# Long self-attention units: two exponential instructions each, and the causal mask added by VectorE

## The reference, cut to what matters

```python
sc = jnp.einsum('bqhd,bkhd->bhqk', qi, k).astype(jnp.float32) * scale
mask = kpos[None, :] <= qpos[:, None]
sc = jnp.where(mask[None, None], sc, -jnp.inf)
p = jax.nn.softmax(sc, axis=-1).astype(v.dtype)
return jnp.einsum('bhqk,bkhd->bqhd', p, v)
```

## Time and profile before

| what | value |
|---|---|
| median of three runs | 2906.83 us |
| the profiled execution | 2907.68 us |
| its span, first to last instruction | 2905.5 us |
| TensorE matmuls, busy | 2851.7 us, 98% |
| VectorE busy | 1533.3 us, 53% |
| ScalarE busy | 860.8 us, 30% |
| GpSimd busy | 1555.7 us, 54% |
| mean granted TensorE clock | 0.998 |
| attention stage of the first layer | about 197 to 405 us of the span |
| attention stage of the second layer | about 1634 to 1843 us |

### The profile page before, as it was taken

The page is one execution under the profiler, slowest core; times in us unless marked ns, Lnnn a source line. Parts: engine busy times, 40 slices in busy tenths (PEclk is TensorE's granted clock), DMA queues, the critical chain, the costliest instruction groups (busy, mean ns, idle before and its releaser), DMA issues.

```text
span 2905.5 us, 36839 instructions
## 1 busy us (share of the span) xinstructions
PE 2851.7 (98%) x13294; PEld 2224.1 (77%) x13294; DVE 1533.3 (53%) x1949; ACT 860.8 (30%) x1440; POOL 1555.7 (54%) x1153
## 2 busy tenths in 40 slices
PE   8999999999999999999999999999999999999998
PEld 6766668886878888888887666688878788888886
DVE  8585556014565445554685755650246555545555
ACT  3455553223321111110224655432324111101113
POOL 4333333441487777777644224334315877777776
PEclk9999999999999999999999999999999999999999
DMA  3100011220111111111111000113101111111112
GB/s 135 48 10 5 16 37 51 87 88 15 44 44 58 47 41 56 58 47 43 60 61 37 14 1 16 44 51 109 59 22 44 40 54 58 51 43 50 58 54 77
DMA packets 61423, 140.37 MB, mean 48 GB/s; under 512 B 9232, under 2 KB 11280, under 8 KB 60688
## 3 DMA queue, kind: packets, MB, share of 16 engines
q1 hardware_dynamic: 61328, 139.06, 14.2%
HBM read 134.58 MB, written 4.46 MB: 48 GB/s over the span
## 4 chain that ended last, share of the span: by engine, by line
PE 86%; DVE 6%; POOL 3%; ACT 2%; issue 2%; DMA 1%; SPq 0%; POOLq 0%; DVEq 0%; ACTq 0%
PE ps L1357 23%; PE ps L1341 19%; PE ps L845 17%; PE ps L1213 6%; PE ps L1067 4%; PE ps L1097 2%; PE ps L1269 2%; PE ps L1293 2%; PE ps L1083 2%; PE ps L1228 1%; PE ps L961 1%; PE ps L1244 1%; DVE xbc L1852 1%; PE ps L1163 1%; POOL ring L751 1%
## 5 line engine op out<-in xcount | busy, mean ns | idle before, releaser
L1357 PE MATMUL ps<-hm_h,ring 128*128 128x512 f32 x2048 | 640.8, 391 | 4.5 <-DVE hm_l L2171 4.4
L2179 DVE TENSOR_TENSOR x<-ps,x 128x512 f32<-128x512 f32 x512 | 352.3, 690 | 273.9 <-PE ps L1357 273.3
L748 POOL TENSOR_TENSOR ring<-raw,ones 128x512 fp32r<-128x512 f32 x334 | 349.9, 1048 | 260.6 <-PE ps L1357 204.3
L1357 PEld LDWEIGHTS ps<-hm_h,ring 128*128 128x128 f32 x2048 | 384.5, 188 | 96.9 <-issue 16.5
L751 POOL TENSOR_TENSOR ring<-raw,ring 128x512 fp32r<-128x512 f32 x334 | 433.1, 1297 | 26.1
L845 PE MATMUL ps<-hA,wsp 128*128 128x512 f32 x1920 | 443.2, 392 | 1.1 <-POOL wsp L603 1.0
L600 POOL TENSOR_TENSOR wsp<-raw,ones 128x1024 fp32r<-128x1024 f32 x63 | 124.4, 1974 | 566.7 <-PE ps L845 454.6
L845 PEld LDWEIGHTS ps<-hA,wsp 128*128 128x128 f32 x1920 | 360.4, 188 | 82.0 <-issue 6.3
L1357 PE MATMUL ps<-hm_l,ring 128*128 128x512 f32 x1024 | 398.9, 390 | 0.0
L1341 PE MATMUL ps<-hT,ring 128*128 128x512 f32 x1440 | 331.9, 390 | 0.9 <-POOL ring L751 0.7
L1341 PEld LDWEIGHTS ps<-hT,ring 128*128 128x128 f32 x1440 | 270.3, 188 | 57.6 <-POOL ring L751 1.7
(11 more groups left out here) (308 smaller groups left out, 3940.2 us busy)
## 6 DMA issues: line engine op xcount, KB each, us to landing
raw<-in_weight_tiles SPq DMA_DIRECT2D x248, 256.0 KB, 2.6
raw<-in_weight_tiles SPq DMA_DIRECT2D x108, 512.0 KB, 3.2
outT<-x SPq DMA_DIRECT2D x16, 256.0 KB, 2.2
x<-in_xT SPq DMA_DIRECT2D x3, 1024.0 KB, 10.2
wh<-in_head_weights SPq DMA_DIRECT2D x8, 256.0 KB, 2.7
raw_early<-in_weight_tiles SPq DMA_DIRECT2D x4, 512.0 KB, 3.7
mem_s<-in_memT SPq DMA_DIRECT2D x2, 1024.0 KB, 4.8
x<-in_xT SPq DMA_DIRECT2D x2, 512.0 KB, 5.3
```

Source lines behind the costliest of these rows:

```text
L748: pool.tensor_tensor(ring[:, slot, 0, :], blk(i), ones[:, 0:1].to_broadcast([P, HT]), ALU.mult).then_inc(op_ready[slot], 1)
L1357: last = pe.matmul(ps[:, bank, :], w[:, part, k, (m % 2) * P:(m % 2 + 1) * P], h[k][:, cols_of(half)], start=(k == 0 and part == 0 and h i ...
L2179: dve.tensor_tensor(xm, ps[:, bank, :], xm, ALU.add).then_inc(x_add, 1)
```

## The change: what it does

It touches the long units alone.

- `scores`: the mask's product (L1070) is left out for them.
- `row_max`: VectorE first adds `future` to the diagonal square in PSUM, 128 by 128, in place, and then (after a `link`) reduces.
- `probs`: the first 512 columns and the rest are two ACTIVATEs. The first sums into a new tile `esum_4` and raises a new semaphore `s_exp_4`; the second sums into `esum` and raises `s_exp`.
- `probs_T`: the first chunk (4 squares) of a long unit waits for `s_exp_4`, the second for `s_exp`.
- `recip_sums`: for the long half of the blocks the two partial sums are first added (128 by 8) and linked.

```diff
+def long_units(n):
+    return sum(unit(m)[1] >= 4 for m in range(n))
...
         esum_4 = at("esum_4", G2 + 4096, [P, 2, NBLK // 2])
...
-                            edge = j + 4 > i
+                            edge = j + 4 > i and i < 4
...
-                        pe.wait_ge(s_exp, here(s_exp, n + 1))
                         for part, j0 in enumerate(range(0, i + 1, 4)):
+                            if part == 0 and i >= 4:
+                                pe.wait_ge(s_exp_4, here(s_exp_4, long_units(n + 1)))
+                            else:
+                                pe.wait_ge(s_exp, here(s_exp, n + 1))
...
-                        act.activation(prob[:, n % 2, 0:w], banks(2 * (n % 2))[:, 0:w], ACT.Exp,
+                        first = 0
+                        if w > HT:
+                            first = HT
+                            act.activation(prob[:, n % 2, 0:HT], ps[:, 2 * (n % 2), :], ACT.Exp,
+                                           bias=stat(nmx, n), accum_out=stat(esum_4, n)).then_inc(s_exp_4, 1)
+                        act.activation(prob[:, n % 2, first:w], banks(2 * (n % 2))[:, first:w], ACT.Exp,
                                        bias=stat(nmx, n), accum_out=stat(esum, n)).then_inc(s_exp, 1)
...
                         w = (unit(n)[1] + 1) * P
+                        diagonal = banks(2 * (n % 2))[:, w - P:w]
+                        if unit(n)[1] >= 4:
+                            link(dve.tensor_tensor(diagonal, diagonal, future[:, :], ALU.add))
                         dve.tensor_reduce(stat(nmx, n), banks(2 * (n % 2))[:, 0:w], AX.X, ALU.max, negate=True).then_inc(s_max, 1)
...
                         dve.wait_ge(s_exp, here(s_exp, 8 * hf + 8))
+                        if hf % 2:
+                            link(dve.tensor_tensor(esum[:, :, 4:NBLK], esum[:, :, 4:NBLK], esum_4[:, :, :], ALU.add))
```

More of the change, by code:

```diff
@@ L172 @@
              "softplus_a": 2, "norm_done": 3, "bc_done": 6, "act_done": 8, "gate_done": 4, "lru_a": 4, "first_qk_act": 8,
-             "k_rope": 2, "k_rope_1": 2, "v_done": 8, "s_exp": 64, "side_act": 42, "pt_sb": 96, "mix_hi": 6, "mix_ln": 1, "mix_gt": 4, "mix_rstd": 3, "mg_hi": 1,
+             "k_rope": 2, "k_rope_1": 2, "v_done": 8, "s_exp": 64, "s_exp_4": 32, "side_act": 42, "pt_sb": 96, "mix_hi": 6, "mix_ln": 1, "mix_gt": 4, "mix_rstd": 3, "mg_hi": 1,
              "xk_done": 8, "mv_done": 2, "xs_exp": 8, "xpt_sb": 8, "xo_hi": 16, "sum_y": 4, "sum_hi": 16, "hm_sq": 64,
@@ L337, in trunk @@
         att_h = at("att_h", o + 824, [P, NBLK, SH], F32R)
+        esum_4 = at("esum_4", G2 + 4096, [P, 2, NBLK // 2])
         cst_r = sem("constants_r")
@@ L376, in trunk @@
         s_ps, s_max, s_exp, pt_ps, pt_sb, o_ps = (sem(n) for n in ("s_ps", "s_max", "s_exp", "pt_ps", "pt_sb", "o_ps"))
+        s_exp_4 = sem("s_exp_4")
         r_inv, y_done, y_sq, y_acc = sem("r_inv"), sem("y_done"), sem("y_sq"), sem("y_acc")
```

## The result

The changed kernel takes 2925.01 us, the median of four runs (2923.49 to 2925.45), against 2906.36 for the kernel before measured beside it: a ratio of 1.006, 95% interval 1.0048 to 1.0072. The forecast was 2919.3, in 2909 to 2927, slower. So direction and range held, and the size was 12.5 us where 18.65 came. The profiled execution took 2923.49 us; its span is 2921.2, 15.7 over the span before.

What follows compares the result with a forecast made beforehand. TensorE bounds the kernel, through its waits on ScalarE's copies behind the exponential. Per layer 3 x 1.31 + 2.32 = 6.25 us, two layers 12.5, giving a median of 2919.3 us, range 2909 to 2927.

Steps and rivals of the forecast that it cites:

- m = 0.06: Mask product taken from TensorE in each long unit: gains 0.06 us on the chain, kept at 0.06 to 0.16.
- a = 0.32: VectorE's add ahead of the row max: costs 0.29 plus 0.03 for the link, 0.32 us, bounds 0.21 to 0.45.
- s = 0.24: Exponential split in two on ScalarE: adds 0.24 us, the fixed part of a slot, bounds 0.19 to 0.37.
- 3(a + s) - 6m a pair: Delay of each of a layer's first three pairs: three add-and-split costs less six saved mask products, 1.31 us.
- starting at 0 before unit 8: Start of the sum for the first three pairs: TensorE's delay against the old timeline is 0 before unit 8.
- Unit 11's wait, released by `probT`: TensorE's transposes of unit 11 carry new idle time of 0.8 to 0.9 us, waiting for ScalarE's copy of unit 10.
- the slack of 0.01: Room at unit 11's transposes over the 0.73 us from copy start to transposes: 0.01 us, so nearly all delay passes on.
- 5a + 4s - 4m in the last pair, 2.32: Delay of each layer's last pair, where fewer side tasks let the loop bind earlier: 2.32 us.
- s is pure cost: The split can't start the first chunk earlier, as it waits for the previous unit's copy, queued behind both halves.
- Rival 3, the clock: Longer waits drop TensorE to 1.2 GHz near 387 or at other pair ends, up to 1.6 us each; chance 0.10.
- Rival 1 (hidden): Slacks at units 10 to 13 hide the delay, only units 14 and 15 pay: 0 to +4 us; chance 0.15.
- rival 2 (faster): First chunk at units 14 and 15 starts after the first half exponential, 0.43 earlier: 2901 to 2894 us; chance 0.07.

Runs made afterwards that it cites:

- the doubled step: The changed kernel with a second linked 128x128 VectorE instruction (the square copied onto itself) behind the add: 2932.46 us, 1.0083 of the kernel before.

## Why the prediction was right, and where its size was off

- *TensorE's waits decide, and they hang on latency, not on the load of ScalarE or VectorE:* right. Both have 40% and more of idle time in the window after, and the pair grew all the same.
- *m = 0.06:* right, 0.066 on average by the kernel without a mask.
- *a = 0.32:* right. The add takes 0.298, and 0.33 to 0.34 from start to start with its link. The unlinked copy of the earlier trace rows, 0.29 long, has its successor 0.21 behind its start; that an unlinked add would overlap in the same way was not tested. The Trainium skill, "VectorE: DVE Perf Modes", "The DRAIN you can't avoid", says that a semaphore between VectorE instructions costs nothing extra. These rows speak against it: by that rule a would be 0.21, and it is 0.33 to 0.34.
- *s = 0.24:* right. At unit 14 above the two halves and the copy behind them start at 295.09, 295.76 and 296.43, 0.67 apart each, as one of 512 columns did in the earlier trace rows; together 1.34 against 1.10 for one of 1024.
- *3(a + s) - 6m a pair:* this is the term that was mis-sized: 1.31 forecast, 1.65 measured. The step that failed is its start, "starting at 0 before unit 8", and the sentence that units 8 and 9 have more room. The output products at unit 8 wait for the copy of unit 7, which is behind the exponential of unit 8. The prediction counted this wait in the last pair and not in the first three, where the old trace has hardly any room either. The copy of unit 7 and the products, ScalarE's and TensorE's timelines, before and then after:
```profile
270.60 0.58 ACT L1599 ACTIVATE probT<-ps 128x512 f32<-128x512 f32 x1
271.43 1.73 PE L1097 MATMUL ps<-probT,v_tok 128*64 128x256 f32 x16
...
272.74 0.58 ACT L1614 ACTIVATE probT<-ps 128x512 f32<-128x512 f32 x1
273.38 1.73 PE L1107 MATMUL ps<-probT,v_tok 128*64 128x256 f32 x16 [0.48 <-ACT probT L1614]
```
The products start 0.83 behind the start of the copy before and 0.64 after, so the slack was 0.19. The four turns that the doubled step shows are at units 8, 10, 11 and 15. Counted after the event, with that slack, the masks of units 10, 13, 14 and 15, and the 0.2 that TensorE gains back at unit 12, 4(a + s) - 4m - 0.4 = 1.6.
- *Unit 11's wait, released by `probT`:* right in size and step, wrong in name. 0.81 us stand at the product of EA, behind ScalarE's EL, which is in the same queue behind the same exponential; the copy was the next one, as moving EL ahead showed. The old trace had it: the product started 0.64 behind the start of EL, as it does after (284.44 and 285.08), and the slack of 0.01 was read one instruction too late.
```profile
281.39 0.59 ACT L1580 ACTIVATE EL<-ps 128x512 f32<-128x512 f32 x1
282.03 0.50 PE L1007 MATMUL ps<-aU_hi,ones_r 128*128 128x512 f32 x1
```
- *5a + 4s - 4m in the last pair, 2.32:* right, 2.2 in both layers once the low clock is taken out.
- *"s is pure cost", since the first chunk's bank is freed behind both halves:* right for this kernel, but the reason was too narrow. With the copy moved to VectorE the first chunk does start early, and the split still costs 0.66 a pair (52.38 against 51.72). Three readers still wait for the end of the second half: EL, the copy of unit 7, and the copy that frees the bank of the next second chunk.
- *Rival 3, the clock:* it came in part. The low clock adds 4.2 us in the profiled execution: it begins eight transposes earlier at the end of both layers, and there is one new place in the second layer, at the wait of 1.8 that the prediction named (measured 1.89). That this place is hit in one layer and not in the other, after the same wait, no row explains. The other pairs' ends, though their waits grew, kept the full clock. Rival 1 (hidden) and rival 2 (faster) fell.

In numbers: the forecast of 12.5 lacks 6 x 0.34 = 2.0 for the fourth turn, net of the slack, and 4.2 for the clock, which the forecast left to rival 3. The last pairs take 0.2 less, the stretch between the layers' attention 0.4 less, and the late load in the profile of the kernel before takes another 2.3 off. That makes the 15.8 between the profiled executions. Without the late load it would be 18.1 of the 18.65. So the mechanism of the forecast held, and about a third of what came was not in its sum. The part by the clock can't be given for the medians, only for these two executions; the mean granted clock was 0.995 to 0.996 in all four of the changed kernel, and 0.998 in the profiled one before.

## What to carry to other kernels

When an instruction on an in-order engine gets longer or gains a predecessor, list everything that stands behind it in that queue and who waits for it: here the copy that frees the bank, a side task and the last copy ahead of the output products, three kinds of reader behind the exponential, and the pair's cost was the added latency times the number of turns, less the slack that was there once. In none of these kernels did the split pay: it can only where someone can use the first half and nobody important waits for the second. To shorten such a loop, move the readers to an engine with idle time rather than the work ahead of them: one copy in four on VectorE and two side tasks ahead of the exponential were worth 12 us, two thirds of what the change costs.

## What was not expected of the hardware

The low clock doesn't follow from the waits alone. In the kernel with the add only, the last output products of both layers ran at the full clock; its chain of waits has them as follows, although this kernel waits longer than the one before ahead of its 24 output products (1.80 for 1.18) and as long, 0.74, ahead of these, which took 5.10 before.
```profile
403.17 3.46 PE ps L1097 x32
...
1843.60 3.46 PE ps L1097 x32
```
They come and go between executions of one kernel too: the seven of this one took 2910.36 to 2919.09 us, with a mean granted clock of 0.999 in the fastest and 0.995 in the slowest. So some 1.6 us at each such place are not tied to an edit, and differences of a few microseconds in the totals above are not to be read as its effect; the length of a pair is the steadier measure.
